# Masking attention scores on the tensor engine, and new start addresses for the activation tensors, in a two-block transformer kernel

## The reference, cut to what matters

```python
        z = jnp.einsum("bqhd,bkhd->bhqk", qb, kb) * scale
        mask = s_idx < t_idx
        log_beta = jax.nn.log_sigmoid(z)
        log_one_minus = jnp.where(mask, jax.nn.log_sigmoid(-z), 0.0)
        tail = lax.cumsum(log_one_minus, axis=3, reverse=True) - log_one_minus
        weights = jnp.where(mask, jnp.exp(log_beta + tail), 0.0)
        outs.append(jnp.einsum("bhqk,bkhd->bqhd", weights, vb))
```

```python
        x = x + (gate * val) @ w_down[layer]
```

## Time and profile before

| | us |
|---|---|
| median of 3 timed runs (lowest, highest) | 1370.53 (1369.76, 1371.23) |
| the profiled execution | 1378.61 |
| its span, from the first to the last instruction | 1376.8 |
| PE busy in the span | 1273.2 (92%) |
| DVE, ACT, POOL busy | 609.8, 476.2, 565.6 |
| mean granted PE clock, as a share of full speed | 0.945 |

### The profile page before, as it was taken

One profiled execution on the slowest core, in us unless ns is written; L12 is line 12 of the kernel. 1 busy time (PEld: TensorE's weight loads), 2 busy tenths in 40 slices (PEclk: granted clock), 3 DMA queues, 4 the chain that ended last, 5 costly groups with the idle time before them and its releaser, 6 DMA issues.

```text
span 1376.8 us, 15496 instructions
## 1 busy us (share of the span) xinstructions
PE 1273.2 (92%) x5620; PEld 1016.8 (74%) x5620; DVE 609.8 (44%) x836; ACT 476.2 (35%) x678; POOL 565.6 (41%) x319
## 2 busy tenths in 40 slices
PE   4999388899999999999989888898999999999997
PEld 3886246577888888888867667687788888888886
DVE  6599845512544544400051546794254544441002
ACT  4332124533433333311133562342433333332213
POOL 4452133135444444444446222542644444444442
PEclk8999657899999999999989999999999999999999
DMA  5231010002332222322213110100233223322211
GB/s 188 80 105 61 0 61 1 1 4 89 99 115 91 91 91 91 114 100 92 91 61 90 41 62 31 62 31 32 92 90 93 91 93 91 120 92 92 91 61 62
DMA packets 84433, 104.80 MB, mean 76 GB/s; under 512 B 1979, under 2 KB 77098, under 8 KB 84394
## 3 DMA queue, kind: packets, MB, share of 16 engines
q1 hardware_dynamic: 84234, 104.01, 23.3%
q10 hardware_dynamic: 160, 0.26, 0.1%
HBM read 101.90 MB, written 2.10 MB: 76 GB/s over the span
## 4 chain that ended last, share of the span: by engine, by line
PE 76%; DVE 9%; issue 7%; ACT 4%; POOL 2%; SPq 1%; DVEq 1%; DMA 0%; POOLq 0%; ACTq 0%
PE ps L1454 17%; PE ps L1251 16%; PE ps L1253 15%; PE ps L1252 15%; PE ps L1615 3%; DVE cy L930 2%; PE ps L1354 2%; PE ps L1568 2%; PE ps L1315 1%; PE ps L1334 1%; POOL htmp L453 1%; ACT w_hi L540 1%; DVE sp_lo L981 1%; PE ps L1298 1%; PE ps L1373 1%
## 5 line engine op out<-in xcount | busy, mean ns | idle before, releaser
L397 POOL TENSOR_TENSOR w_lo<-w_raw,w_hi 128x1024 fp32r<-128x1024 f32 x190 | 462.1, 2436 | 600.6 <-ACT w_hi L540 600.4
L1251 PE MATMUL ps<-h_hi,w_hi 128*128 128x512 f32 x1040 | 414.1, 398 | 10.5 <-DVE h_lo L887 5.3
L1252 PE MATMUL ps<-h_lo,w_hi 128*128 128x512 f32 x1040 | 408.9, 393 | 0.0
L1253 PE MATMUL ps<-h_hi,w_lo 128*128 128x512 f32 x1040 | 408.8, 393 | 0.0
L540 ACT ACTIVATE w_hi<-w_raw 128x1024 fp32r<-128x1024 f32 x190 | 199.4, 1054 | 335.1 <-PE ps L1454 171.2
L1251 PEld LDWEIGHTS ps<-h_hi,w_hi 128*128 128x128 f32 x1040 | 197.6, 190 | 57.3 <-issue 15.3
L1253 PEld LDWEIGHTS ps<-h_hi,w_lo 128*128 128x128 f32 x1040 | 197.7, 190 | 42.4
L1252 PEld LDWEIGHTS ps<-h_lo,w_hi 128*128 128x128 f32 x1040 | 198.1, 191 | 40.7 <-issue 0.5
L988 DVE TENSOR_TENSOR xT<-xT,ps 128x512 f32<-128x512 f32 x32 | 22.0, 688 | 282.8 <-PE ps L1454 228.2
L1454 PE MATMUL ps<-a_hi,w_hi 128*128 (+1 forms) x352 | 139.5, 396 | 0.0
L1454 PE MATMUL ps<-a_lo,w_hi 128*128 (+1 forms) x352 | 139.5, 396 | 0.0
(11 more groups left out here) (230 smaller groups left out, 1312.9 us busy)
## 6 DMA issues: line engine op xcount, KB each, us to landing
w_raw<-in_w_up SPq DMA_DIRECT2D x33, 1024.0 KB, 5.1
w_raw<-in_w_down SPq DMA_DIRECT2D x22, 1024.0 KB, 4.8
w_raw<-in_w_in SPq DMA_DIRECT2D x21, 1024.0 KB, 5.3
w_raw<-in_w_gate SPq DMA_DIRECT2D x11, 1024.0 KB, 5.3
w_raw<-in_w_out SPq DMA_DIRECT2D x8, 1024.0 KB, 4.9
xtok<-in_x SPq DMA_DIRECT2D x2, 1024.0 KB, 6.0
out_dram<-obuf SPq DMA_DIRECT2D x8, 256.0 KB, 2.9
kT<-kT ACTq DMA_DIRECT2D x2, 128.0 KB, 2.3
```

What stands on the lines that cost most here:

```text
L397: pool.tensor_tensor(unit_view(w_lo, at, down), unit_raw(at, down), unit_view(w_hi, at, down).bitcast(F32), ALU.subtract).then_inc(s_lo, 1)
L1251: pe.matmul(ps[:, bank, :], whi, hi[:, k, :], start=first, stop=False, skip_group_check=True)
L1252: pe.matmul(ps[:, bank, :], whi, lo[:, k, :], start=False, stop=False, skip_group_check=True)
L1253: mm = pe.matmul(ps[:, bank, :], wlo, hi[:, k, :], start=False, stop=last, skip_group_check=True)
```

## The change: masks by matmul, and one padded tensor for the small ones

After the four score matmuls of a head, PE adds the causal mask to the diagonal blocks by three matmuls whose stationary operand is an identity matrix and whose moving operand is the mask: 0 where it is open, -1e30 where it is closed. Column 0 takes one block, column 512 two blocks side by side, column 1024 one. `s_z`, for which ACT's Abs waits, is now raised by the last of these. DVE's two multiplications by `smask` and its two clamp-and-mask instructions in PSUM are gone, together with their semaphore; ACT's final Exp now waits for the tails themselves. A masked score of -1e30 gives max(z, 0) = 0 and ln(1 + exp(-1e30)) = 0, and exp of the masked sum gives 0.

The small tensors become columns of one tensor of 256 bytes, `gq8` too, and `lbt` grows from 96 to 128 bytes. With that `sq`, `cy`, `qk`, `zl`, `sp_hi`, `sp_lo`, `m_hi`, `m_lo`, `a_hi`, `a_lo` and `cv` begin at 128 modulo 256; `sm`, `ee`, `acc`, `kd`, `qs` and `off` begin at 0. `xT`, `h_hi`, `h_lo` and the weights stay where they were. DVE prepares the identity and the doubled mask (two copies) at the start; POOL has one memset and one select fewer.

```diff
-        stat = sb("stat", [P, 4])
-        rstd = sb("rstd", [P, 4])
-        ss0 = sb("ss0", [P, 4])
-        sinkb = sb("sinkb", [P, 8])
-        mhalf = sb("mhalf", [P, 4])
+        small = sb("small", [P, 64])
+        stat, rstd, ss0, mhalf = (small[:, 4 * n:4 * n + 4] for n in range(4))
+        sinkb, gq8 = small[:, 16:24], small[:, 24:25]
...
-            gq8 = sb("gq8", [P, 1], stack=early)
             lnone = sb("lnone", [P, P], stack=early)
-            smask = sb("smask", [P, P], stack=early)
             nmask = sb("nmask", [P, P], stack=early)
+            nmask2 = sb("nmask2", [P, 2, P], F32R, stack=early)
+            identr = sb("identr", [P, P], F32R, stack=early)
...
-            lbt = sb("lbt", [P, 6, 4], stack=mid)
+            lbt = sb("lbt", [P, 8, 4], stack=mid)
...
                 if 1 <= s <= AH:
-                    act.wait_ge(s_dm, 2 * s)
+                    act.wait_ge(s_tail, s)
                     act.activation(zl[:, (s - 1) % 3, :], zps(s - 1), ACT.Exp).then_inc(s_w, 1)
...
+            dve.tensor_copy(identr[:], ident[:]).then_inc(s_cdve, 1)
+            dve.tensor_copy(nmask2[:], nmask[:, None, :].to_broadcast([P, 2, P])).then_inc(s_cdve, 1)
...
-                if 1 <= s <= AH:
-                    dve.wait_ge(s_tail, s)
-                    three, one = blocks(zps(s - 1))
-                    dve.scalar_tensor_tensor(three, three, 0.0, nmask[:, None, :].to_broadcast([P, 3, P]),
-                                             ALU.min, ALU.add).then_inc(s_dm, 1)
-                    dve.scalar_tensor_tensor(one, one, 0.0, nmask[:], ALU.min, ALU.add).then_inc(s_dm, 1)
...
                     link(dve.scalar_tensor_tensor(z, zps(s), 0.0, z, ALU.max, ALU.add), s_sp)
-                    three, one = blocks(z)
-                    dve.tensor_tensor(three, three, smask[:, None, :].to_broadcast([P, 3, P]), ALU.mult).then_inc(s_sp, 1)
-                    counts[s_sp] += 1
-                    link(dve.tensor_tensor(one, one, smask[:], ALU.mult), s_sp)
...
                 for b in range(4):
-                    mm = pe.matmul(zps(h)[:, ZOFF[b]:ZOFF[b] + ZLEN[b]], qk[lo:lo + 64, 4 + j, b * P:(b + 1) * P],
+                    pe.matmul(zps(h)[:, ZOFF[b]:ZOFF[b] + ZLEN[b]], qk[lo:lo + 64, 4 + j, b * P:(b + 1) * P],
                                    qk[lo:lo + 64, j, b * P:SEQ], start=(b != 3), stop=False, skip_group_check=True)
+                for at, n in ((0, 1), (ZOFF[3], 2), (ZOFF[2], 1)):
+                    mm = pe.matmul(zps(h)[:, at:at + n * P], identr[:], nmask2[:, 0:n, :].rearrange("p a n -> p (a n)"),
+                                   start=False, stop=False, skip_group_check=True)
                 mm.then_inc(s_z, 1)
```

More of the change, by code:

```diff
@@ L195, in hybrid_blocks_kernel @@
         s_tail = sem("s_tail")
-        s_dm = sem("s_dm")
         s_w = sem("s_w")
@@ L368, in _ @@
             pool.memset(lnone[:], 1.0 / (CT * P)).then_inc(s_const, 1)
-            pool.memset(smask[:], 1.0).then_inc(s_const, 1)
             pool.memset(nmask[:], 0.0).then_inc(s_const, 1)
@@ L372, in _ @@
             pool.memset(glu[:, :, 0:PAD], 0.0).then_inc(s_const, 1)
-            pool.wait_ge(s_const, 11)
+            pool.wait_ge(s_const, 10)
             pool.affine_select(out=sel[:], in_=sel[:], compare_op=ALU.is_ge, fill=0.0, base=0,
@@ L378, in _ @@
                                pattern=[[P, 8], [1, P]], channel_multiplier=-64).then_inc(s_const, 1)
-            pool.affine_select(out=smask[:], in_=smask[:], compare_op=ALU.is_gt, fill=0.0, base=0,
-                               pattern=[[1, P]], channel_multiplier=-1).then_inc(s_const, 1)
             pool.affine_select(out=nmask[:], in_=nmask[:], compare_op=ALU.is_gt, fill=NEG, base=0,
@@ L386, in _ @@
                                pattern=[[-1, P]], channel_multiplier=1).then_inc(s_const, 1)
-            pool.wait_ge(s_const, 16)
+            pool.wait_ge(s_const, 14)
             pool.affine_select(out=sel[:], in_=sel[:], compare_op=ALU.is_ge, fill=0.0, base=63,
@@ L859, in link @@
                 dve.wait_ge(s, counts[s])
-            dve.wait_ge(s_const, 16)
+            dve.wait_ge(s_const, 14)
             dve.tensor_copy(ntri[:], ntri_f[:]).then_inc(s_cdve, 1)
             dve.tensor_scalar(nones[:], ones[:], -1.0, None, ALU.mult).then_inc(s_cdve, 1)
+            dve.tensor_copy(identr[:], ident[:]).then_inc(s_cdve, 1)
+            dve.tensor_copy(nmask2[:], nmask[:, None, :].to_broadcast([P, 2, P])).then_inc(s_cdve, 1)
             for m in range(KD):
@@ L942, in _ @@
             link(dve.tensor_tensor(nvar[:, 1, :], nvar[:, 1, :], nvar[:, 2, :], ALU.mult), s_qv)
-            dve.wait_ge(s_cdve, 3)
+            dve.wait_ge(s_cdve, 5)
             for j in range(8):
@@ L948, in _ @@
                                          ALU.mult, ALU.mult).then_inc(s_qn, 1)
-            def blocks(t):
-                return t.rearrange("p (a n) -> p a n", n=P)[:, 0:9:4, :], t[:, ZOFF[1]:ZOFF[1] + P]
             for s in range(AH + 3):
@@ L1381, in convolution_part @@
                     unit_mms(OUT_BANK[m], U_OUT + m, k, k == 4, False)
-            pe.wait_ge(s_cdve, 2)
+            pe.wait_ge(s_cdve, 4)
             for s in range(AH + 2):
```

## The result

The changed kernel takes 1349.99 us (median of 4 runs, 1349.29 to 1350.67), the kernel before beside it 1370.82 us (4 runs, 1369.76 to 1371.23): ratio 0.985, 95% interval 0.983 to 0.987, 20.8 us less. The forecast was 1348.5 us. Run again later in five rounds, the changed kernel took 1352.5 us (1349.38 to 1354.35; ratio 0.986, 0.984 to 0.988). The forecast's total came out, in part by luck: its largest term was 6 us too high, and half-speed stretches of PE elsewhere, which come and go from run to run, made up for most of that.

What follows compares the result with a forecast made beforehand. PE was taken to bound the kernel, by its pace where full and its waits in the first attention. 1370.5 less 22.0 us (14.2 attention, 7.8 addresses) gave 1348.5 us, range 1341 to 1361.

Steps and rivals of the forecast that it cites:

- its largest term: First block's attention: masks moved from DVE to PE gain 18.3 us less 4.1 for clock falls, 14.2 us.
- the stage's length before: First block's attention in the profiled execution: six heads from about 201.2 to 273.64 us, some 12.1 us each.
- the stage's new end: ACT's table load behind head 6 in the attention: at 255.4 us in place of 273.6, before falls of the clock.
- The 4.1 us for falls within the heads: Attention: one to two falls of PE's clock, from new gaps when DVE's splits run long, 4.1 us together.
- a clock above 0.85: Sign in the changed kernel's profile: PE's clock between about 201 us and the table load behind head 6.
- Taking these 1.6 us off the serial loop: Attention: DVE's four mask instructions alone give only 11 us; DVE's wait for the tails goes too, opening the loop.
- The masks on PE: Three mask matmuls per head in the attention: 0.37 us at full clock, 0.74 at low, 0.6 for the first head.
- The operand's place decides: Second products and second output projection: the moving operand's start modulo 256 sets the pace, 6.6 ns a matmul, 7.8 us.
- Rival (a): Second products: the addresses do nothing, something else slows `a` and `m`; 1356.3 us, chance 0.13.
- (b): Attention: the clock falls in each head's scores, returning only in the tails, 12.2 us a head; 1362.7 us, chance 0.15.
- (c): Attention: PE stays at the low clock from s = 2 to 7, 15.4 us a head; slower, 1384 us, chance 0.04.
- (d): Attention: POOL's layer-norm chain holds PE at s = 3, or ACT's Silu; stage gain 10 us, 1352.7 us, chance 0.08.

Runs made afterwards that it cites:

- e4: Changed kernel, with DVE again waiting for the tails of head s-1 ahead of the softplus of head s: 1352.87 us, ratio 0.986.
- e7: Changed kernel with rows of a_hi and a_lo 32 bytes longer and the weights beginning at 32 modulo 256 in place of 128: 1373.98 us, ratio 1.001.
- e12: Changed kernel with DVE's wait for the tails and its clamp and mask in PSUM kept, only the two 0/1 mask multiplications gone: 1353.49 us, ratio 0.987.
- e6: Changed kernel with each row of a_hi and a_lo 32 bytes longer, so tile k begins at 128 + 32k modulo 256, weights at 128: 1357.38 us, ratio 0.989.
- e11: Changed kernel with 32 floats more in lbt, putting the second block's moved tensors back to 128 modulo 256: 1350.47 us, ratio 0.986.
- e1: The kernel before, unedited, run once more for a second trace: 1371.17 us, span 1369.4.
- e10: Changed kernel with unread matmuls before the first scores, 12 ahead of the eight q/k-norm broadcasts and three behind each: 1354.29 us, ratio 0.990.

## Why the prediction was right, and where it was wrong

**The sum.** 22.0 us were foreseen and 20.8 measured. Both traces of the changed kernel against the second of before say what it is made of: 7.9 us in the attention, 8.0 in the downs, 0.4 to 0.5 for `m`, together 16.3 to 16.4 us. Another 0.8 to 0.9 us lies ahead of the first scores, where kernels with the same instructions differ by more than that. The rest, 4.7 us in the first trace, is what half-speed stretches elsewhere happened to give; in the second trace it is 0.4. So it is luck that the total came within 1.2 us: the attention's term was 6.3 us too high, and some 5.5 us that nothing shows to be the change's stood in for it. In the later rounds the medians lie 18.6 us apart.

**The step that failed: the stage's length before.** "Six heads take from about 201.2 to 273.64, some 12.1 us each", and "I take the difference over as it is" for the 8.1 us by which the profiled execution lay above the median. Those 8.1 us were not spread over the program. The second trace of before, at the median, has 7.4 us less in the very stage that the change shortens, and all other stages the same. The gain was worked out against an unusually long attention (102.7 us) and subtracted from a median that belongs to a usual one (95.3): 14.2 us were foreseen, 7.9 came. Against the first trace it would be 15.3, so that the term looked right there. Put well, the sum would have taken the stage's new end from the median execution: the table load at 266.25 becomes 255.99, 10.3 us with the earlier start, less 1.5 behind it.

**The stage's new end.** It was worked out at 255.4 us unhindered and 259.5 with one to two falls of the clock inside. Measured: 255.99. The beat of 8.0 to 8.2 us was right (8.3 and 8.0 us from head 4 to 6), and so were the beats with the sums and the broadcast (8.7 and 9.2, foreseen 9.1 and 9.5), the first head (final Exp ends at 201.44, foreseen 201.2) and PE at s = 3, which doesn't wait for POOL's chain. The 4.1 us for falls within the heads didn't come: from 211 to 256 us the clock is 1.00. The fall came behind the last scores, where the outputs of head 6 wait for the Silu, and cost 1.5 us. The sign "a clock above 0.85" between 201 us and the table load held: it is 0.91 over 201 to 256 us, though half speed lasts until 211.

**The mechanism of the attention.** "Taking these 1.6 us off the serial loop would give only 11 us. But the wait goes too, so the loop itself opens." The wait's going gave 0.3 us (e4 against e7), and the clamp's and the wait's together 1.9 to 3.6 us (e12 against the changed kernel and e7). The serial loop was 8.4 us when undisturbed, half a microsecond above the 7.9 us that PE's queue takes with the masks. Taking 0.82 us out of it was enough to make PE the bound in the later heads; in the first ones, where DVE's splits are long, the rest of the relief counted too. The gain is largest where the old loop was disturbed: 3.0 us from head 1 to 2, where DVE's splits of 1.6 and 2.45 us stood on the path, which are now hidden.

**The masks on PE.** 0.49 us in place of 0.37 at the full clock, 0.84 in place of 0.6 to 0.74 at half. It went into the beats without harm. At the start they took more of PE, which the prediction didn't have. In the timeline of the kernel before, the 16 score matmuls of the first two heads take 7.79 us as one group, at half speed:

```profile
182.28 7.79 PE L1343 MATMUL ps<-qk 64*128 64x512 f32 x16 [0.84 <-DVE qk L947]
```

With the masks of head 0 between them they take 10.03 us (181.47 to 191.50), 1.4 us more than the masks' 0.84 explain. It is hidden here, since the first tails wait for DVE's splits: they start 13.3 us after the first scores in both kernels.

**The addresses.** 4.0 us in each down, 8.0 for 1056 matmuls in both, that is 7.6 ns each and not 6.6: the old pace was taken too low, from a count in a stretch (233.2); by the starts in the first trace of before it is 39.36 us for 168 matmuls (650.03 to 689.39 us), 234.3 ns, and the new one is 226.7. And 0.4 to 0.5 us for `m`, not 0.8. "The operand's place decides" was right for this kernel and too simple as a rule: it is the distance from the weights' start (e6, e7). That the slow pace outlasts the slow operand by some matmuls was right as well (e6). Rival (a) fell, and with it the bound of 0.

**The rivals.** (b) and (c) fell: scores take 4.6 us in the first three heads and 2.4 us in the other five. (d) fell. No run shows a cost of what moved in the second block (e11), as foreseen.

## What to carry to other kernels

Take a second trace of the kernel before, and compare it with the first stage by stage, before a stage's length goes into a sum: an excess of the profiled execution over the median usually has a place, and it may be the one that you are about to shorten. Where two engines' loops are within a few per cent of each other, taking a small instruction off the longer one may give most of what there is. To see what each part gives, compare traces in which the stage was granted the same clock. Place the moving operand of fp32r matmuls at the same start modulo 256 bytes as the stationary one: here this is 3% of PE's time in a stage that PE bounds (119.0 us in place of 123.0), for less than 256 bytes a partition.

## What the runs showed of the hardware that was not expected

- The pace of 128x128 by 512 fp32r matmuls depends on the distance of the two operands' starts modulo 256 bytes: 226.7 ns at 0, 229 at 64, 233 to 234 at 32, 96, 128, 160, 192 and 224 (e6, e7). The direction counts: a moving operand 64 bytes above the weights' start is nearly as fast as one at 0, one 64 below is slow (234 and 233). Behind slow matmuls the first five at distance 0 are still slow, 232 ns each (e6).
- Two executions of one program can differ by 7.4 us in one stage and agree in all others within 0.1 us. The runs of the kernel before that stood beside e1 spread from 1369.67 to 1378.88 us, those of the masks alone sat at 1357.6 or at 1364.3.
- PE busy 22.0 of 24 us was granted 0.50 throughout, and the full clock, once reached through added matmuls, was lost again at 180.5 us while PE ran without a gap from 162.5 to 197.8 us (e10).
- The 64-row score matmuls of the first two heads, directly behind each other, took 7.79 us at half speed in the kernel before, less than twice one group's 4.63: the second head's first began at 185.43 us, 1.1 us before the first head's last. With three 128-row matmuls between the groups this was gone.
